# Compressed attention scores: gate first into a tile of their own and turn them from there, normalize in place behind it

## The reference, cut to what matters

```python
s_c = jnp.einsum('bqgjd,bngd->bqgjn', q_blk, k_cmp) - slopes[:, :, None] * dist_c
p_c = masked_softmax(s_c, (dist_c >= 0)[None, :, None, None, :])
o_c = jnp.einsum('bqgjn,bngd->bqgjd', p_c, v_cmp)
imp = jnp.einsum('bqgjn,nm->bqgm', p_c, cover)
...
o = g_blk[:, :, 0, :, :, None] * o_c + g_blk[:, :, 1, :, :, None] * o_s + g_blk[:, :, 2, :, :, None] * o_w
```

## Time and profile before

| | |
|---|---|
| median of 3 runs | 3056.48 us (3055.37 to 3062.33) |
| the profiled execution | 3056.54 us, span 3054.8 us |
| PE busy | 2926.3 us, 96% of the span |
| DVE, ACT, POOL busy | 1224.2, 955.2 and 1408.5 us |
| mean granted clock of TensorE | 0.985 of full |
| the 80 steps with compressed scores among them | from about 1655 to 1965 us |

### The profile page before, as it was taken

How to read it: one execution, slowest core, us unless ns; L and a number is a source line. 1 busy time by engine, 2 the same in 40 slices (tenths; PEclk the granted TensorE clock), 3 DMA queues, 4 the chain that set the end, 5 groups by cost and what they waited for, 6 DMA issues and landing times.

```text
span 3054.8 us, 43415 instructions
## 1 busy us (share of the span) xinstructions
PE 2926.3 (96%) x17327; PEld 2355.6 (77%) x17327; DVE 1224.2 (40%) x2021; ACT 955.2 (31%) x1626; POOL 1408.5 (46%) x920
## 2 busy tenths in 40 slices
PE   6998899989999999999899898999999999999998
PEld 4887877877888888888787666666687888888887
DVE  5455463523431231232401677645514331331334
ACT  3434442332330120121201655777713320210211
POOL 1445534655444444444433555545535444444442
PEclk9999999989999999999999999999999999999999
DMA  4110011021111111111420000000011111111112
GB/s 142 42 29 2 16 35 42 22 83 42 55 48 48 48 46 46 52 46 51 115 69 28 1 2 1 1 1 8 8 39 45 48 48 48 48 44 53 48 44 73
DMA packets 212558, 127.57 MB, mean 42 GB/s; under 512 B 9016, under 2 KB 208189, under 8 KB 212285
## 3 DMA queue, kind: packets, MB, share of 16 engines
q1 hardware_dynamic: 210797, 125.32, 14.0%
q10 hardware_dynamic: 1616, 0.21, 0.0%
HBM read 112.94 MB, written 8.39 MB: 40 GB/s over the span
## 4 chain that ended last, share of the span: by engine, by line
PE 84%; DVE 6%; ACT 4%; issue 2%; POOL 2%; DMA 0%; SPq 0%; DVEq 0%; ACTq 0%; POOLq 0%
PE PS L1907 56%; PE PS L2569 4%; PE PS L2590 4%; PE PS L2208 3%; PE PS L2643 3%; PE PS L2609 3%; ACT X L1167 1%; PE PS L2050 1%; PE PS L1949 1%; DVE X L1536 1%; DVE X L1809 1%; DVE X L1325 1%; PE PS L1935 1%; ACT Z L1179 1%; PE PS L2060 1%
## 5 line engine op out<-in xcount | busy, mean ns | idle before, releaser
L501 POOL TENSOR_TENSOR WH<-WR,ONES 128x1024 fp32r<-128x1024 f32 (+1 forms) x192 | 452.2, 2355 | 1156.0 <-PE PS L1907 981.5
L1907 PE MATMUL PS<-YH,WH 128*128 128x512 f32 x1888 | 586.2, 392 | 5.3 <-POOL WL L504 4.1
L1907 PE MATMUL PS<-YH,WL 128*128 128x512 f32 x1888 | 582.8, 390 | 0.0
L1907 PE MATMUL PS<-YL,WH 128*128 128x512 f32 x1888 | 582.8, 390 | 0.0
L504 POOL TENSOR_TENSOR WL<-WR,WH 128x1024 fp32r<-128x1024 f32 (+1 forms) x192 | 456.0, 2375 | 15.1
L1650 DVE SCALAR_TENSOR_TENSOR X<-PS,PTF,X 128x1023 f32<-128x1023 f32 (+1 forms) x176 | 225.7, 1282 | 561.5 <-ACT X L1120 548.7
L1907 PEld LDWEIGHTS PS<-YH,WH 128*128 128x128 f32 x1888 | 354.6, 188 | 81.8 <-POOL WL L504 4.5
L1907 PEld LDWEIGHTS PS<-YL,WH 128*128 128x128 f32 x1888 | 355.3, 188 | 74.5
L1907 PEld LDWEIGHTS PS<-YH,WL 128*128 128x128 f32 x1888 | 355.3, 188 | 74.1
L1120 ACT ACTIVATE X<-PS,PTF 128x1024 f32<-128x1024 f32 x88 | 106.2, 1207 | 829.5 <-PE PS L1907 823.3
L741 POOL TENSOR_SCALAR X<-X,STAT,SM 128x640 f32<-128x640 f32 (+6 forms) x215 | 179.6, 845 | 171.8 <-DVE STAT L1820 171.7
(11 more groups left out here) (408 smaller groups left out, 3970.9 us busy)
## 6 DMA issues: line engine op xcount, KB each, us to landing
WR<-in_ffn_w_up_dram SPq DMA_DIRECT2D x88, 512.0 KB, 3.8
WR<-in_hy_w_in_dram SPq DMA_DIRECT2D x28, 512.0 KB, 3.8
WR<-in_ffn_w_down_dram SPq DMA_DIRECT2D x32, 448.0 KB, 3.5
WR<-in_ffn_w_down_dram SPq DMA_DIRECT2D x16, 512.0 KB, 3.6
WR<-in_nsa_w_in_dram SPq DMA_DIRECT2D x14, 512.0 KB, 3.8
X<-in_x_dram SPq DMA_DIRECT2D x8, 512.0 KB, 7.3
xt_scratch<-H SPq DMA_DIRECT2D x1, 4096.0 KB, 13.3
WR<-in_hy_w_out_dram SPq DMA_DIRECT2D x8, 512.0 KB, 3.7
```

The source lines that it names most:

```text
L501: pool.tensor_tensor(WH[:, slot, 0:k, :], WR[:, slot, 0:k, :], ONES[:, :].unsqueeze(1).broadcast_to([P, k, P]), ALU.mult).then_inc(w_hi, 1)
L1907: ins = pe.matmul(PS[:, 2 * slot + a, :], w[:, slot, i, :], y[:, i, a * HALF:(a + 1) * HALF], start=(i == 0 and w is WH and y is hi), stop ...
```

## The change

POOL's two operations on a compressed step are exchanged in role. DVE now multiplies the reciprocals by the gates into a third row of `CST` (8 numbers in each partition, one new small operation behind the reciprocal). POOL's first operation multiplies the exponentials by that product into `CPN`, which is now the gated tile, and PE turns the heads from `CPN` once this one operation is done. POOL's second operation normalizes the exponentials in place, and DVE's importance sum reads them from there and waits for the second operation instead of the first.

Two guards follow from it. POOL may write `CPN` again only when PE has turned the previous compressed step (before: when DVE had summed it). And a place in the ring may be written again only when the importance sum that read it is done, for which `cmp_front` and `bias_step` wait for `imp_c` as well.

```diff
@@ scale_step (POOL)
                     if cmp_no[p]:
-                        pool.wait_ge(scaled, 2 * max(q for q in range(p) if steps[q][0] == 2) + 2)
-                        pool.wait_ge(imp_c, cmp_no[p])
-                    pool.tensor_tensor(CPN, scores_of(p), CST[:, cmp_no[p] % 2, 1, :].unsqueeze(2).broadcast_to([P, JH, NC]),
+                        last = max(q for q in range(p) if steps[q][0] == 2)
+                        pool.wait_ge(scaled, 2 * last + 2)
+                        pool.wait_ge(tr_done, pair_groups[last + 1])
+                    pool.tensor_tensor(CPN, scores_of(p), CST[:, cmp_no[p] % 2, 2, :].unsqueeze(2).broadcast_to([P, JH, NC]),
                                        ALU.mult).then_inc(scaled, 1)
                     pool.wait_ge(scaled, 2 * p + 1)
-                    pool.tensor_tensor(scores_of(p).rearrange("p (e m) n -> p e m n", e=2), CPN.rearrange("p (e m) n -> p e m n", e=2),
-                                       GATE[:, qt, h:h + JH].rearrange("p (m e) -> p e m", e=2).unsqueeze(3).broadcast_to([P, 2, JH // 2, NC]),
+                    pool.tensor_tensor(scores_of(p), scores_of(p), CST[:, cmp_no[p] % 2, 1, :].unsqueeze(2).broadcast_to([P, JH, NC]),
                                        ALU.mult).then_inc(scaled, 1)
@@ cmp_front and bias_step (DVE)
                 if scores_free[p]:
                     dve.wait_ge(tr_done, pair_groups[scores_free[p]])
+                    if cmp_no[scores_free[p]]:
+                        dve.wait_ge(imp_c, cmp_no[scores_free[p]])
@@ cmp_back (DVE)
-                dve.reciprocal(rs, rs).then_inc(r_ready, 1)
+                link(dve.reciprocal(rs, rs))
+                dve.tensor_tensor(scale.rearrange("p (e m) -> p e m", e=2), rs.rearrange("p (e m) -> p e m", e=2),
+                                  GATE[:, qt, h:h + JH].rearrange("p (m e) -> p e m", e=2), ALU.mult).then_inc(r_ready, 1)
@@ cmp_sum (DVE)
-                dve.wait_ge(scaled, 2 * p + 1)
-                dve.tensor_reduce(out=IMPP[:, (h // JH) * TT + qt, 1:1 + NC], in_=CPN.rearrange("p h n -> p n h"), op=ALU.add,
+                dve.wait_ge(scaled, 2 * p + 2)
+                dve.tensor_reduce(out=IMPP[:, (h // JH) * TT + qt, 1:1 + NC], in_=scores_of(p).rearrange("p h n -> p n h"), op=ALU.add,
                                   axis=AX.X).then_inc(imp_c, 1)
@@ turn (PE)
-                        pe.wait_ge(scaled, 2 * p + (2 if b == 2 else k + 1))
-                    src = scores_of(p)[:, (k % 2) * 4 + k // 2, :] if b == 2 else score_buf(p, k % 2, (k // 2) * P, (k // 2 + 1) * P)
+                        pe.wait_ge(scaled, 2 * p + (1 if b == 2 else k + 1))
+                    src = CPN[:, (k % 2) * 4 + k // 2, :] if b == 2 else score_buf(p, k % 2, (k // 2) * P, (k // 2 + 1) * P)
```

More of the change, by code:

```diff
@@ L1731, in cmp_back @@
             def cmp_back(p):
-                rs = CST[:, cmp_no[p] % 2, 1, :]
+                b, h, qt = steps[p]
+                rs, scale = CST[:, cmp_no[p] % 2, 1, :], CST[:, cmp_no[p] % 2, 2, :]
                 dve.wait_ge(p_ready, 2 * p + 2)
```

## The result

| | before | after |
|---|---|---|
| median (runs) | 3056.48 us (5: 3053.36 to 3062.33) | 3071.16 us (5: 3070.30 to 3074.67) |
| ratio, 95% interval | | 1.0048 [1.0037, 1.0059] |
| the profiled execution | 3056.54 us | 3074.37 us |
| mean granted clock in it | 0.985 | 0.979 |

Executions of most kernels fall into two groups some 5 us apart (of the kernel before at about 3056 and 3062, with mean granted clocks of 0.985 and 0.982), so means over many executions are given further down beside the medians.

A forecast was written before the change was run, and what follows sets the result against it. PE, busy for 96% of the span, was taken to bound the kernel. Delays passed on to PE at the compressed steps summed to +3.8 us on 3056.54, giving 3060.4 us, with a range of 3052 to 3067.

The forecast's parts named there:

- Step 25: Compressed step: PE turns 0.91 us earlier, but the late importance sum delays the next step's scalings; PE ends +0.55 us.
- steps 4 and 5: Neighbouring compressed steps: the second one's importance sum slips 2.4 us, delaying a bias and PE's later scores by +1.0 us.
- The second chain through DVE: Importance sum, next reciprocal, two POOL scalings, PE transposes: a sum 0.62 us late returns the 0.91 gain and loses 0.55.
- the size of PE's gain: PE's turn of a compressed step, released by POOL's first operation: 0.91 us earlier in the worked-through pattern.
- The sum of +3.8: All delays passed on to PE over the compressed steps, added up: +3.8 us on the profiled execution.
- Steps 45 and 57: First: PE waits for a bias behind the new DVE operation; second: DVE's queue is late only by it; +0.2 us each.
- step 49: Compressed step where DVE is late itself, so its queue slips only by the new operation's 0.20 us: +0.2 us.
- rival C: Slower for the same reason: more PE idleness in total calls up one or two half-clock stretches; 3064 to 3068, chance 0.22.
- Rival B: Clock in the compressed stage: a shortened PE wait wins back half of 36 us at half clock; 3053, chance 0.14.
- Rival A: The chain through DVE has slack, so PE's waits on compressed steps shrink and the gain stays; 3051, chance 0.08.

The follow-up runs named there:

- e7: The kernel after, but PE waits for POOL's second operation again before turning a compressed step; median 3064.57 us, ratio 1.0033.
- e10: The kernel before plus the new small DVE operation (result unused) and the importance sum waiting for POOL's second operation; median 3062.47 us, ratio 1.0019.
- e1: The kernel after with DVE's importance sum placed behind the next step's reciprocal in its queue; median 3055.53 us, ratio 0.9983.
- e2: The kernel before with DVE's importance sum placed behind the next step's reciprocal in its queue; median 3052.03 us, ratio 0.9983.
- e5: The kernel before plus only the new small DVE operation, its result unused; median 3056.35 us, ratio 0.9997.
- e6: The kernel before, with only the importance sum made to wait for POOL's second operation; median 3055.00 us, ratio 0.9992.
- e11: e1 plus 5 superfluous identity matmuls in PE's waits at each of six compressed steps; median 3056.36 us, ratio 0.9999.
- e8: The kernel after plus superfluous identity matmuls in PE's waits, 5 at six compressed steps and 7 at the step behind each; median 3056.80 us, ratio 1.0005.

## Why the prediction was wrong in size and right in sign

By its own steps, the two traces aligned at PE's instructions. PE comes to the attention 0.6 us late in this execution, a difference that is none of the change's; each step then adds:

| step | forecast | measured | PE late by, then |
|---|---|---|---|
| 4, 5 | +1.0 | +1.0 | 1.58 |
| 9 | +0.1 | not to be read, a half-clock stretch covers it | |
| 17 | +0.55 | -0.91, then +1.50: +0.59 | 3.96 |
| 25 | +0.55 | -0.91, then +1.45: +0.54 | 4.58 |
| 33, 37 | +0.4 | +0.46 | 5.04 |
| 41 | +0.2 | -1.20, then +1.44: +0.24 | 5.28 |
| 45 | +0.2 | +0.75 | |
| 49 | +0.2 | +0.46 | |
| 53 | +0.2 | not to be read, a half-clock stretch covers it | |
| 57 | +0.2 | +0.70 | 12.75 |
| 61 | +0.2 | none | |

The third column is the change of PE's lateness at the step, the last one the lateness behind it. Step 25 can be followed in the timeline above, and the 12.75 in the rows of steps 57 and 58 (1902.98 - 1890.22). For steps 4 and 5 the scores of step 9 start at 1693.86 after, and at 1692.28 before.

- **The second chain through DVE, "the core of the forecast"**: right, to 0.02 us at step 25. So was the new operation at 0.168 us, and the size of PE's gain.
- **The sum of +3.8**: the steps that can be read add to 4.7 (1.0 + 0.59 + 0.54 + 0.46 + 0.24 + 0.75 + 0.46 + 0.70), for 3.3 forecast at the same ones. Steps 45 and 57 were mis-sized by 0.5 each and step 49 by 0.3; why is not shown.
- **What failed is the clock.** The sum left it as it was, a term put at nothing in the forecast, and rival C priced "one or two more stretches of 10 us at 1.2 GHz" at "4 us each: 3064 to 3068". The profile has 27 us more of it in this stage (61 less 34), and the executions have 27 more in the mean. Of the 17.5 us by which PE is late at the end of the stage, 0.6 came with it and 4.7 are the chain; 12.2 are left, 0.45 us for each of the 27. The stretches themselves agree: in the one that begins at 1842.0 after (13.7 us) PE's lateness grows from 5.5 to 11.1 us, 0.41 for each. The price of a stretch was about right. What was mis-sized is how much of it there would be: 27 us, near three times 10, and not one or two.
- **Why C got 0.22.** I set against it that "PE idles more in total". It idles 1.5 us more in 328, so the sum of the idleness was the wrong measure: e7 idles more still, and is faster with less time at half clock. Rival B expected that halving the 2.30 us wait of step 41 would win clock back, and the clock went the other way. Its own counter-argument, "the idleness comes back a step later, in two parts", is what the trace shows, with 36 idle pieces over 0.3 us for 29. That this is what brought the clock down is argued from e7, and e10 does not fit a count of pieces.
- **Rival A** (the gain stays) fell as said: the second chain had no slack. Even where that chain is taken away (e1 against e2) the gain is 0.6 +- 1.3 us the wrong way.

**What stays open.** Taken over whole executions the clock explains 8 us (27 x 0.30) and 7 remain at equal clock; taken over the aligned stage it is 12 and 5. The difference is in what a us at half clock is worth, 0.30 over everything and some 0.45 here, where PE is nearly always the bound; no run fixes it. Which arrangement of waits brings the clock down is open: e7 and after differ in it as a count of pieces would have it, e10 and before do not. And why e5 and e6 are free alone is not shown.

## What to carry to other kernels

Follow a released wait one step on: if a reduction that nobody is in a hurry for stands in the same queue ahead of a reciprocal that the next step needs, the release comes back as a wait there; put the hurried one first (worth 4 us here before any other change, and 19 after it). With PE over 90% busy, read the granted clock of the stage beside the waits, and look at how the idleness is spread as well as at its sum; an earlier release that only brings a second wait a step later can cost more than it gives (some 5 to 7 us here, e7). Where PE must wait, a few superfluous matmuls in the wait can pay for themselves (6.8 and 14.5 us here), but measure how long one takes and how long the wait is: in e11 five took 1.11 us in a wait of 0.51, and it was no gain.

## What the runs showed of the hardware

- Matmuls whose result is written over, put into PE's waits, raised the granted clock: with 72 of them (144 in the trace, in a stage that has some 2,500 without them) the time at half clock went from 124 to 81 us an execution, and with 54 in the kernel before from 97 to 77. In e11, 30 of them changed nothing in it (99 and 100).
- A matmul of the identity with itself, 128 by 128 in float32, is two matmuls in the trace and takes 0.22 us of PE at full clock (ten rows from 1759.89 to 1761.00 in e8).
- One us at half clock went with 0.30 us in the mean of the whole kernel, and with some 0.41 to 0.45 in the stage in which PE is the bound.
- At nearly equal busy time of PE in ten us (7.1 and 7.2), the ten us behind were granted 1.00 in the kernel before and 0.52 in the one after; PE's waits for POOL were one of 2.07 us with two short ones in the first, and three of 0.84 to 0.91 in the second. That is one place.
- A two-input operation on DVE with 8 numbers in each of 128 partitions takes 0.166 to 0.170 us, and starts 0.03 us behind the reciprocal that feeds it.
